# A hybrid retention and RG-LRU decoder block on one core: the value product as seven half-size products for each pair of heads

## The reference

```python
h = rms_norm(x, in_norm_g)
q, k, v, g, xr, gr, m_ret, m_rnn = split(h @ w_in)      # w_in: 1024 x 10240; v is 4 heads x 512 columns
o = head_norm(retention(rot(q), rot(k), v))             # chunks of 128 tokens
y_ret = (silu(g) * o) @ w_ret_o
xr = causal_depthwise_conv(xr)                          # 4 taps
r = sigmoid(xr_block @ w_a + b_a)                       # 4 blocks of 256 channels: the recurrence gates
i = sigmoid(xr_block @ w_i + b_i)
a = exp(-8 * r * softplus(-a_param)); u = sqrt(1 - a*a) * i * xr
hr = scan(h[t] = a[t] * h[t-1] + u[t])
y_rnn = (hr * gelu(gr)) @ w_rnn_o
x = x + (sigmoid(m_ret) * y_ret + sigmoid(m_rnn) * y_rnn) @ w_out
x = x + (silu(gate) * val) @ w_down                     # gate, val = conv3(rms_norm(x) @ w_up)
```

## Time and profile before

| what | value |
|---|---|
| median of 3 runs | 1988.98 us (1988.25 to 1992.77) |
| profiled execution | span 1988.8 us |
| PE busy | 1961.3 us (99%) |
| DVE busy | 1418.8 us (71%) |
| ACT busy | 934.4 us (47%) |
| POOL busy | 333.9 us (17%) |
| chain that ended last | PE 83%, DVE 9%, ACT 3%, DMA 2%, issue 2%, POOL 1% |

### The profile page before, as it was taken

One profiled execution on the slowest core, in us unless ns is written; L12 is line 12 of the kernel. 1 busy time (PEld: TensorE's weight loads), 2 busy tenths in 40 slices (PEclk: granted clock), 3 DMA queues, 4 the chain that ended last, 5 costly groups with the idle time before them and its releaser, 6 DMA issues.

```text
span 1988.8 us, 24558 instructions
## 1 busy us (share of the span) xinstructions
PE 1961.3 (99%) x9208; PEld 1639.4 (82%) x9208; DVE 1418.8 (71%) x1621; ACT 934.4 (47%) x1182; POOL 333.9 (17%) x277
## 2 busy tenths in 40 slices
PE   8999999999999999999999999999999999999998
PEld 6888888888888888888888787997888888888887
DVE  7877876776755445667777658658987888776766
ACT  6443353343445555555555443346544544543335
POOL 2000010010392000067775003100000000000000
PEclk9999999999999999999999999999999999999999
DMA  6343554445697443465668555532222222256523
GB/s 259 117 169 137 180 181 157 169 158 179 206 327 281 159 159 127 148 200 173 206 190 256 199 196 194 184 112 84 85 91 78 84 84 84 74 191 234 199 96 132
DMA packets 222205, 325.07 MB, mean 163 GB/s; under 512 B 11824, under 2 KB 150448, under 8 KB 221872
## 3 DMA queue, kind: packets, MB, share of 16 engines
q1 hardware_dynamic: 196800, 232.84, 35.5%
q0 software_dynamic: 22608, 85.99, 11.0%
q10 hardware_dynamic: 2720, 5.24, 0.8%
HBM read 223.36 MB, written 100.66 MB: 163 GB/s over the span
## 4 chain that ended last, share of the span: by engine, by line
PE 83%; DVE 9%; ACT 3%; DMA 2%; issue 2%; POOL 1%; ACTq 0%; SPq 0%; DVEq 0%; POOLq 0%
PE ps L346 27%; PE ps L348 27%; PE ps L347 27%; DVE ws L329 1%; DMA stg<-scr_y 1%; DMA raw<-scr_q 1%; PE ps L1219 1%; POOL qkvs L949 1%; POOL state_s L955 1%; DVE ysr L2415 0%; DVE wx L2155 0%; POOL ws L968 0%; DVE wsr L2408 0%; ACT ri L1648 0%; DVE th L2337 0%
## 5 line engine op out<-in xcount | busy, mean ns | idle before, releaser
L1501 ACT ACTIVATE wx<-raw 128x1024 fp32r<-128x1024 f32 (+1 forms) x152 | 137.3, 905 | 252.3 <-DVE raw L2131 131.4
L346 PE MATMUL ps<-xs,wx 128*128 128x512 f32 x612 | 239.1, 391 | 2.1 <-DVE xs L2578 1.6
L348 PE MATMUL ps<-xs,wx 128*128 128x512 f32 x612 | 238.3, 389 | 0.0
L347 PE MATMUL ps<-xs,wx 128*128 128x512 f32 x612 | 238.2, 389 | 0.0
L2155 DVE TENSOR_TENSOR wx<-raw,wx 128x1024 fp32r<-128x1024 f32 (+1 forms) x152 | 158.9, 1047 | 30.4 <-ACT wx L1501 30.2
L346 PE MATMUL ps<-sc,wx 128*128 128x512 f32 x448 | 174.4, 389 | 0.0
L348 PE MATMUL ps<-sc,wx 128*128 128x512 f32 x448 | 174.3, 389 | 0.0
L347 PE MATMUL ps<-sc,wx 128*128 128x512 f32 x448 | 174.3, 389 | 0.0
L1536 ACT ACTIVATE ub<-ps 128x512 f32<-128x512 f32 x112 | 66.9, 597 | 159.1 <-PE ps L348 156.4
L346 PEld LDWEIGHTS ps<-xs,wx 128*128 128x128 f32 x612 | 114.9, 188 | 28.4 <-issue 2.7
L348 PEld LDWEIGHTS ps<-xs,wx 128*128 128x128 f32 x612 | 114.9, 188 | 24.1
(11 more groups left out here) (289 smaller groups left out, 4849.2 us busy)
## 6 DMA issues: line engine op xcount, KB each, us to landing
raw<-w_in SPq DMA_DIRECT2D x80, 512.0 KB, 5.5
scr<-ost POOLq DMA_DIRECT2D x32, 1024.0 KB, 5.2
raw<-w_up SPq DMA_DIRECT2D x44, 512.0 KB, 4.2
tq<-w_down SPq DMA_DIRECT2D x88, 128.0 KB, 2.7
scr_t<-tq POOLq DMA_DIRECT2D x22, 512.0 KB, 3.2
scr_h<-vt POOLq DMA_DIRECT2D x11, 1024.0 KB, 4.3
tr<-w_ret_o SPq DMA_DIRECT2D x64, 128.0 KB, 3.9
scr_q<-tr POOLq DMA_DIRECT2D x16, 512.0 KB, 5.2
```

Source lines behind the costliest of these rows:

```text
L346: pe.matmul(out, w(HI), x(HI), start=first, stop=False, skip_group_check=True)
L347: pe.matmul(out, w(HI), x(LO), start=False, stop=False, skip_group_check=True)
L348: return pe.matmul(out, w(LO), x(HI), start=False, stop=last, skip_group_check=True)
L1501: act.activation(dst, src, ACT.Copy).then_inc(sem["f_hi"], 1)
```

## The change

The value product is also done by seven half-size products, for two heads at a time (g = 0, 1): the quarters are token half x feature half, and feature half x head. That makes 2 x 7 products of 2 chunks of 24 matmuls, `value(i)` for i = 0 to 27, so 672 matmuls in place of 768. The gates of recurrence block n come behind chunk 7n+3. The sums of the value weights are formed in 16 more pieces through the same `tq`, one in each of blocks 8 to 23 at a new place in DVE's list (place 0, in the middle of the block; the old place at the end is place 1), and go to `scr_w`. The activations' sums are stored to `scr_s` in block 3, and come back chunk by chunk (`v_sums`). The partial results are kept in the accumulators c11, c12, c21 and c22 (`vacc`; ACT's `v_copy` starts one, DVE's `v_add` adds to it), of which c11, c21 and c22 lie where `tr` was. Chunk weights go through three split buffers `vws`. The recurrence's element-wise work is cut in two halves m = 0, 1 (`decay`, `driven`, `scan`).

```diff
+V_CHUNKS = 28
+V_PIECES = 16
+PIECES = sorted([(_b, 1, "down", _j) for _j, _b in enumerate(W_AT)] + [(_b, 0, "value", _j) for _j, _b in enumerate(range(8, 8 + V_PIECES))])
+V_W = ["b21", "b11", "t2", "t3", "t4", "t1", "b22"]
+V_GATES = 3
...
             for b in range(IN_BLOCKS + 2):
-                load_in(b)
+                if b < IN_BLOCKS:
+                    load_in(b)
+                elif b == IN_BLOCKS:
+                    sp_.wait_ge(sem["f_lo"], in_prepared(b - 2, "b22"))
+                    sp_.wait_ge(sem["tq_out"], 16 * len(PIECES))
+                    v_weights(0)
+                    v_weights(1)
...
-                if b - 1 in W_AT:
-                    load_tq(W_AT.index(b - 1))
+                load_piece(b - 2, 1)
+                load_piece(b - 1, 0)
...
+            recurrence_loads(0)
+            v_weights(2)
+            v_weights(3)
+            for n in range(3):
+                v_sums(n)
...
             for b in range(IN_BLOCKS):
-                if b in W_AT:
-                    store_tq(W_AT.index(b))
+                store_piece(b, 0)
+                store_piece(b, 1)
...
+            def v_bank_free(g, p, t):
+
+                if p == 0 and g:
+                    pe.wait_ge(sem["v_ad"], 16 * g - 4 + t + 1)
+                elif p in (1, 3):
+                    pe.wait_ge(sem["v_cp"], 16 * g + (0 if p == 1 else 4) + t + 1)
+                elif p == 4:
+                    pe.wait_ge(sem["v_cp"], 16 * g + 8 + 2 * t + 2)
+                elif p:
+                    pe.wait_ge(sem["v_ad"], 16 * g + {2: 0, 5: 4, 6: 8}[p] + t + 1)
...
+            for i in range(V_CHUNKS):
+                value(i)
+                if i % 7 == V_GATES:
+                    gates(i // 7)
...
+            v_w_hi(2)
+            in_out(IN_BLOCKS - 1)
+            act.wait_ge(sem["sp_st"], 1)
+            act.activation(sp[:, 1, :], sp[:, 0, :], ACT.Exp).then_inc(sem["sp_st"], 1)
             for n in range(LRU_BLOCKS):
...
+                if n:
+                    v_w_hi(first + 2)
+                if odd:
+                    v_copy(n // 2, 3, ("c21", "c22"))
+                v_w_hi(first + 3)
+                if not odd:
+                    if n == 0:
+                        for v in range(4):
+                            act.wait_ge(sem[f"tr_out{v}"], 16 * R_PIECES // 4)
+                    v_copy(n // 2, 0, ("c11",))
+                v_w_hi(first + 4)
...
                     combine_t4(b + 1, 1 - u, 0, in_prepared(b + 1, "b1"))
                     prep_lo(b + 1, 1 - u, "t4", in_prepared(b + 1, "t4"))
+                    combine_piece(b, 0)
...
                 in_c(b, u, 3)
-                if b in W_AT:
-                    combine_down(W_AT.index(b))
+                combine_piece(b, 1)
...
+                driven(n, 0)
+                scan(n, 0)
+                if n < 3:
+                    v_w_lo(first + 8)
+                driven(n, 1)
+                if odd:
+                    v_add(n // 2, 6, "c12")
+                scan(n, 1)
```

More of the change, by code:

```diff
@@ L239, in build @@
     tq, _ = at("tq", [P, 4, BC], F32, A21 + 12 * K1)
+    vws = [at(f"vws{u}", [P, 2, 2, HALF], F32R, WS + 8 * u * K1)[0] for u in range(3)]
+    vss = [at(f"vss{u}", [P, 2, 2, HALF], F32R, o)[0] for u, o in enumerate((WS + 24 * K1, WS - 8 * K1, C + 8 * K1))]
+    vacc = {n: at("v" + n, [P, 4, HALF], F32, o)[0] for n, o in (("c11", A21), ("c22", A21 + 8 * K1), ("c12", C))}
+    vacc["c21"] = vacc["c11"]
     wsd = [at(f"wsd{u}", [P, 2, 3, HALF], F32R, A + (0, 86)[u] * K1)[0] for u in range(2)]
@@ L300, in build, with kept @@
     ost_ready, stored = [sem["ost0"], sem["ost1"]], [sem["sto0"], sem["sto1"]]
+    def kept(slot, pairs):
+        return stored[slot], 16 * (pairs - (2 + 2 * slot if pairs >= LAST_PAIR else 0))
     def load_block(sp_, pair, slot, first, second):
@@ L722, in _ @@
             for slot in range(2):
-                sp_.wait_ge(stored[slot], 16 * LAST_PAIR)
+                sp_.wait_ge(*kept(slot, LAST_PAIR))
             chunk_load(0)
@@ L893, in store @@
             def store(pair, slot, dst):
-                pool.wait_ge(ost_ready[slot], pair + 1)
+                pool.wait_ge(ost_ready[slot], pair + 1 - (V_PAIRS[1] - V_PAIRS[0] if pair >= LAST_PAIR else 0))
                 pool.dma_start(dst, ost[:, slot, :, :] if dst.shape[1] == 2 else
@@ L941, in _ @@
                                ).then_inc(sem[f"ysto{n % 2}"], 16)
+                if n % 2 == 0:
+                    store_v(n // 2, "c21", 8, sem["vst_a"])
+                    store_v(n // 2, "c22", 12, sem["vst_c"])
+                    store_v(n // 2, "c12", 16, stored[0])
             def store_rnno(n):
@@ L1628, in _ @@
                 act.activation(xcs[:, HI, :, :], xc[:, u, :, :], ACT.Copy).then_inc(sem["x_hi"], 1)
[L1629 to L1637 removed]
+                v_w_hi(first + 5)
+                v_w_hi(first + 6)
+                gate(n, 0, "b_a")
+                gate(n, 1, "b_i")
                 act.wait_ge(sem["gr_evac"], 4 * n + 4)
@@ L1649, in _ @@
                         sem["tanh_done"], 1)
-                split_next(split_hi, act, n)
-                act.wait_ge(stored[1], 16 * i)
-                evac_v(i, 1, range(0, 2))
-                act.wait_ge(sem["om_done"], n + 1)
-                act.activation(ri[:, 0, :, :], ri[:, 0, :, :], ACT.Sqrt).then_inc(sem["sq_done"], 1)
-                evac_v(i, 1, range(2, 4))
+                if n < 3:
+                    v_w_hi(first + 7)
+                if not odd:
+                    v_copy(n // 2, 2, ("c12",))
+                decay_root(n, 0)
+                if n < 3:
+                    v_w_hi(first + 8)
+                else:
+                    act.wait_ge(sem["v_done"], V_CHUNKS - 1)
+                    split_hi(act, LAST_PAIR, 0)
+                decay_root(n, 1)
             def yr_hi(t):
@@ L2365, in rnno_gated @@
                 if job == 0:
-                    dve.wait_ge(stored[slot], 16 * pair)
+                    dve.wait_ge(*kept(slot, pair))
                 if n == 0 or job == 0:
```

482 lines of the change are left out of this document (298 added, 184 removed).

## The result

The changed kernel takes 2086.38 us (median of 4 runs, 2083.72 to 2087.43), the kernel before 1988.97 (1988.25 to 1992.77): a ratio of 1.048, 95% interval 1.0468 to 1.0496. Forecast was 2070, range 2040 to 2098. The profiled execution has a span of 2085.6 us, 96.8 more than that of before.

What follows compares the result with a forecast made beforehand. PE, with work for 1961 of 1989 us, was taken as the bound. The sum was 1988.8 - 21.8 - 1.2 + 64.1 + 18.8 + 2.5 + 13.1 + 6 = 2070.3, so 2070 us, range 2040 to 2098.

Steps and rivals of the forecast that it cites:

- The matmuls saved: Value stage: 768 value matmuls become 672, 96 x 0.2267 = -21.8 us.
- The loop, +64.1: Input projection: four pieces through tq take 46.4 us against 38.1 a pair of blocks, delaying block 24's product 3 by 64.1 us.
- the 8 foretold: Projection, between 260 and 590 us: PE was to pause some 8 us every 46 us.
- Start of the value stage, +18.8: Before chunk 2: weights behind the gates' inputs on SP, then ACT's list, make PE wait 18.8 us.
- Chunk 8 +2.5, chunk 14 +6.6, `LAST_PAIR` +6.5: Value stage waits: bank copies behind chunk 9's high part, 2.5 us; late c12 additions in DVE's list, 6.6 and 6.5.
- Gates, sums and the remaining weights come out in time by the same count: Rest of the value stage: no further waits were expected from these, so no cost was added.
- Clock, +6: Block 24, chunk 2, chunk 14 and LAST_PAIR: a lower clock after each pause, 1.6 us lost each time, +6 us.
- No clock cost in the projection: Projection: its eight pauses, some 13 us by the skill's rule, counted as none, since PE has 8 us spare each turn.
- The 8 MB of sums in block 3, at nothing: Block 3: storing activation sums costs nothing, as raw weights behind are needed a block later; otherwise some 10 us once.
- rival of a *longer* loop: Projection: pauses cost clock on the path and stores behind a block's take 6 us or more; about 2093 us, chance 0.16.
- short end: Projection: DMA serves a piece beside a block's store without delay, 43.7 us a pair, +43 us; 2049 us, chance 0.14.
- faster* rival: Whole kernel: pieces keep up, chunk 2 and c12 come in time, the 96 matmuls come off in full; 1966 us, chance 0.04.

Runs made afterwards that it cites:

- the run with weights first: Changed kernel with SP loading the weights of chunks 2 and 3 ahead of the last w_ret_o piece's loads: 2083.91 us, ratio 1.0463.
- the run with all orders and no pieces: Changed kernel without value pieces (plain columns read instead of sums), value stage's copies, weight loads, splits and c12 additions reordered, tr wait narrowed: 1994.93 us, ratio 1.0018.

## Why the forecast was right in its kind and 16 us low

- **The matmuls saved**: 96 fewer are counted (9112 for 9208). At 0.2267 us each the stage's 864 make 195.9 us. As forecast.
- **The loop, +64.1**: 68.6. In the pair shown the legs agree to 0.3 us each. PE's idle time in that pair is 6.6 us, in two pauses, for the 8 foretold; the rest of the 8 is matmuls at the lower clock. The period was 46.65 (seven pairs from 267.01 to 593.57) for 46.4, which makes 1.8; the end piece of block 9 came at 264.13 for 261.6, which makes the other 2.5.
- **Start of the value stage, +18.8**: 19.3, by the chain named: weights behind the gates' inputs, then ACT's list. The weights of chunk 2 were there 24.1 us into the stage, for 23.3 (2 us of that, for the last 0.5 MB, had no row behind them). The wait for `tr`, on which the chain also named the copies to depend, would have let them go only 6 us sooner (the run with weights first): it stood hidden behind the one forecast.
- **Chunk 8 +2.5, chunk 14 +6.6, `LAST_PAIR` +6.5**: 2.45, 6.60 and 6.53.
- **"Gates, sums and the remaining weights come out in time by the same count"**: this is the step that failed. The first gates waited 3.2 us for the low part of their input. ACT made its high part behind that of chunk 4, whose weights SP had issued behind `v_sums`, which stood still for a block's store: 22.9 us on SP's list, which I had followed only to chunk 3. ACT's row for chunk 4 and SP's for the sums:

```profile
702.99 1.06 ACT L1688 ACTIVATE vws<-raw 128x1024 fp32r<-128x1024 f32 x1 [7.74 <-DMA raw<-scr_w]
```

```profile
673.68 22.92 SPq L616 DMA_DIRECT2D vss<-scr_s  x3
```

  That store itself was late by the cause already named. POOL issued it at 690.73, when ACT had finished the last block in `ost`, and ACT does so behind the high part of chunk 2, whose weights came at 687.44. With the weights first the pause did not go: there POOL issued this store at 681.04, behind its last pieces of `tr`, and SP's list stood still for 18.0 us all the same.
- **Clock, +6**: mis-sized. I priced four restarts at 1.6, and they cost 1.7, 1.5, 2.0 and 2.8. The windows behind the six pauses from 593.5 on (granted clock in the third column from the end):

```profile
593.50:600.00 6.50, 6.43 (x21) 5.16 (x22) 4.88 (x6) 1.12 (x2) 0.54 (x1) 0.74 0.93 309
693.60:700.00 6.40, 6.34 (x22) 5.18 (x23) 3.86 (x19) 1.64 (x3) 0.00 (x0) 0.77 0.55 201
709.30:715.00 5.70, 5.62 (x18) 4.48 (x19) 4.73 (x6) 3.26 (x4) 0.79 (x1) 0.70 0.72 195
746.30:752.00 5.70, 5.64 (x18) 4.51 (x19) 4.23 (x3) 4.33 (x7) 0.70 (x1) 0.70 0.89 309
798.30:805.00 6.70, 6.64 (x21) 5.35 (x22) 4.08 (x4) 0.00 (x0) 0.75 (x1) 0.70 1.03 418
906.00:912.00 6.00, 5.96 (x15) 4.75 (x16) 5.96 (x5) 1.79 (x1) 0.75 (x1) 0.54 0.60 246
```

  Length of the window by one minus the clock gives 1.7, 1.5, 1.7, 1.7, 2.0 and 2.8: 11.4 us, an estimate. The pauses of 2.45 and 3.2 us cost as much as long ones, and I had counted neither. In the value stage the whole loss of this kind is 204.1 of PE busy less 195.9 of matmuls, 8.2 us.
- **No clock cost in the projection**: right. PE is busy for 40.3 of 46.9 us at a mean clock of 0.95, so it makes up the slow stretch inside time that the loop takes anyway. The Trainium skill ("TensorE: Matmul & The Clock Gate", HAM oscillation) says that a loop in which PE waits for transfers starts cold in each turn. Here PE waits for DVE, which waits for the transfers, and the trace agrees in seven of eight turns: behind the pause before product 3 the clock is 0.50 to 0.76 over the next 5 to 7 us, but 1.00 behind that of 547.11. It shows no price for it, since PE is not what the loop waits for.
- **The 8 MB of sums in block 3, at nothing**: without the pieces product 3 of block 24 is at 524.65, where before it was at 525.00. Right.

Together: 4.5 for the loop, 3.2 for the gates, 5.4 for the clock beside the 6 counted, 0.5 for chunk 2: 13.6 of the 15.3 us between the sum and the profiled execution. The rest is spread. The rival of a *longer* loop, at 2093, was nearer in number than the forecast, and had part of the truth (clock on the path, in the value stage), but not its reason: the legs were not longer, and clock in the projection did not count. The legs of the *short end* add up to 43.3 and not to the 43.7 stated, which would have put it at some 2045 for 2049; the runs were far from either. The *faster* rival needed both a loop in 38 us and a value stage that loses under 23: without pieces the first holds, and even then the time was 2010.8, and came to 1987.5 only with the value stage in another order.

## What to carry to other kernels

Before work is added to an engine "with slack", follow the buffer, not the engine: one buffer that is loaded, worked on, stored and reloaded has a least period, and each use of it costs that period however idle the engines are; a store that stands behind one that waits for other work lengthens it. Fewer matmuls pay only if every sum and copy that the form needs is ready in time; here 22 us of matmuls had to carry 16 more trips, 8 MB of stored sums with their reloads, and all the copies and additions of the accumulators. And an earlier transfer gains nothing where the next wait on the same list comes close behind it: read the whole list of the waiting engine, to its end.

## What the runs showed of the hardware

- In the changed kernel a store of 0.5 MB landed in 5.0 us when issued 0.7 us behind a 1 MB store (5.2 had been assumed), and in 3.1 with a 1 MB store behind it. The DMA issues of the changed kernel between 340 and 365 us (KB of one, us to landing):

```profile
scr_w<-tq POOLq DMA_DIRECT2D x1, 512.0 KB, 5.0
...
scr_t<-tq POOLq DMA_DIRECT2D x1, 512.0 KB, 3.1
```

  The Trainium skill ("DMA: Bandwidth & Descriptors", Queues, rings and completion order) says, of the queues of SP and ACT, that the descriptors of one ring are taken up in order, though one may finish before its forerunner. These stores went out on POOL's queue; their times agree with the first, and show nothing on the second.
- At the start of the value stage of the run with all orders and no pieces the 16 DMA engines moved 412 to 419 GB/s over 10 us, at a share of 1.02 to 1.03, and a load of 0.5 MB then took 18.7 us from issue to landing, against 5.5 as the page's median. The Trainium skill ("Perfetto Trace Analysis", Roofline) gives some 435 GB/s for the 16 engines together; what was reached here is 419.
- How long PE had paused does not by itself say whether the clock falls. It fell behind the pause of 2.45 us before chunk 8 (0.70 in the next 5.7 us), and did not behind one of 1.7 us (1.00 in the window behind the pause before `LAST_PAIR` of the run with all orders and no pieces):

```profile
814.60:820.00 5.40, 5.38 (x24) 4.45 (x25) 5.33 (x6) 1.11 (x1) 0.76 (x1) 1.00 0.96 330
```

  But in the projection of the changed kernel it was 1.00 behind pauses of 2.35 us (at 342.16) and 3.47 us (at 575.47), and 0.66 behind one of 1.84 us (at 529.09):

```profile
342.10:347.00 4.90, 4.84 (x21) 4.04 (x22) 4.80 (x10) 2.04 (x4) 0.00 (x0) 1.00 0.00 0
575.40:581.00 5.60, 5.53 (x24) 4.58 (x25) 5.41 (x10) 2.06 (x4) 0.00 (x0) 1.00 0.01 5
529.00:534.00 5.00, 4.91 (x15) 3.88 (x15) 4.90 (x10) 0.79 (x3) 0.00 (x0) 0.66 0.00 0
```

  What decides it was not tried.
